# Sixteen merge-gate units projected in a phase of their own, by seven block products a pair, between the first net and attention

## The chip, the cores and the metric

The kernel runs on one core of a Trainium2 chip. The metric is the device time of one execution in microseconds (us). Below, PE is TensorE, ACT is ScalarE, DVE is VectorE, POOL is GpSimd and SP is SyncE, whose queue issues the kernel's DMAs. L526 is line 526 of the kernel before.

## The reference, cut to what matters

Two transformer blocks run over 1024 tokens of width 1024, in fp32. The first has a hybrid mixer (a state space part and retention) and a gated convolution net of width 2816. The second projects its input `x` once (`z = x @ w_in`) for three branches, gates them and ends in a second net:

```python
(qa, ka, va, qg, kg, vg, glr, gout, qh, fh, ih, hout, mg) = split_columns(x @ w_in)
oa = diff_attention(...)                  # 4 heads
ob = chunked_gated_linear_attention(...)  # GLA, 4 heads, log_g = log_sigmoid(...) / 16
log_f = logaddexp(log(max(lb, floor)), log1p(-lb) + log_sigmoid(fh)); k_h = -expm1(log_f)
oc = chunked_gated_linear_attention(qh, k_h, ih, log_f)   # HGRN, 4 heads
y = einsum('btnc,ncd->btnd', stack(oa, ob, oc), w_branch)
gates = sigmoid(mg.reshape(b, t, 3, 1024))
mix = einsum('btnd,btnd->btd', gates, y) @ w_out
```

`mg` is 3072 columns: 24 tiles of 128 columns by 1024 tokens, called gate units here. They depend on `x` alone, so they can be projected at any time before the branches are merged.

## The kernel before, in words

Every engine has its own program, written by hand and in order; semaphores join them. An fp32 product is three matmuls of cut operands: high by high, low by high and high by low. The cut of an input block is XH and XL. A weight unit of 512 KB goes through a ring: SP loads WR, ACT cuts the high half WH (L1520), POOL the low half WL (L3299), and PE waits for that.

A feature unit (L526) gives 128 columns for 1024 tokens: eight slices of six matmuls, 48 in all. The slices are a generator that `tick` advances, so they are laid between the steps of other work.

The two nets project their upper weights by pairs of units with seven block products instead of eight (`pe_up`, L971): the input is split by rows and tokens into quarters, seven sums and differences of quarters (TH and TL hold the combined ones, numbered 1 to 4) are multiplied by sums and differences of the two units' halves, and ACT and DVE add up the seven results (PC tiles). A pair costs 84 matmuls instead of 96. POOL makes the combined weights (L3333 to L3339) and their low cuts.

The order of the work around the change:

1. The first net's lower product ends with the layer norm of the eight token tiles of XF. DVE norms, ACT scales (L1752), POOL multiplies by the gain (L3353), PE turns XF by transposes (L601), ACT and DVE cut it out of PSUM to XH and XL (L1739, L2624). Then POOL adds the bias for the residual (L3358) and SP stores it.
2. `pe_open` (L867) projects the first head's q, k and v by half tokens, with the turns of x between them.
3. Attention: four heads of eight steps. A step has scores (L1252), transposes of the softmax weights (L1265) and outputs (L1282), and HEAD_TICKS says how many slices stand beside it. The slices are the next head's projections, then gate units from BESIDE_HEAD.
4. Six gated jobs: jobs 0 and 1 have two GLA heads each, jobs 2 to 5 one HGRN head each. A job has levels 0 to 6 of decayed products KQ by KQ (L1397, L1385; DVE makes KQ on L3154 and L3156 out of K, Q and the decays DD) and a diagonal, then eight chunks (state, output), and at last the transposes of the normed output YG (L1447). JOB_TICKS gives the slices before level 0, after each level and after each chunk; what is left is run by `finish(fill)` ahead of the YG transposes. Beside job j run the projections for job j+1: first its keys (ck), which for HGRN are also the forget gates, out of which ACT and DVE compute log_f (L2111, L2085, L2087; L3031, L3018, L3023, L3043); then the output gate of job j, q and v of job j+1, and the gate units of BESIDE_JOB.
5. The branch products, with the late gate units between them, then the output projection and the second net.

A gate unit done early is copied from PSUM to EG by ACT (L1528) and stored to DRAM; it is read back for its sigmoid later.

```python
pe_open(e, [(("dq", 0), "w_in_2", 0), (("dk", 0), "w_in_2", 512), ((("dv", 0), "x"), "w_in_2", 1024)])
...
    fill = chain(pe_gated_keys(e, j + 1), pe_gated_gates(e, j), pe_gated_project(e, j + 1), pe_early(e, BESIDE_JOB[j]))
    compute(j, fill, JOB_TICKS[j])
...
                    last.then_inc(c_o, 1)
                    tick(fill, per[2])
                finish(fill)
                bk.let(uo)
```

Of the kernel before, what the change touches and what calls it, by code (L numbers as in the profile page):

```python
# [294 lines left out]
def build(nc, D, out):  # L295
# [19 lines left out]
    with ExitStack() as ctx:  # L315
# [548 lines left out]
        def pe_half(e, u, wh, wl, h, beside={}):  # L864
            for k in range(8):
# [3 lines left out]
                for what, part in beside.get(k, ()):  # L869
                    pe_turn_pair(e, *what, part)  # L870
            return last

        def pe_open(e, units):

            us = []

            def begin(n):
                name, unit, col = units[n]
                v = wt.next(unit, 0, 8, col, 128)
                us.append((v, claim(e, name, 2, hold=True)))  # L880
# [6 lines left out]
            begin(0)
            pe_wait_pairs(e, "x2", (0, 1))
            first(0)
            begin(1)  # L890
            pe_turn_pair(e, "x2", 2, (0, 1, 2))
            first(1)
            pe_turn_pair(e, "x2", 2, (3,))
            bk.lend(lots["x2n"], ln_ab, chains_of["x2"] + 4)
            begin(2)
            pe_turn_pair(e, "x2", 3, (0, 1))
            first(2, {3: ((("x2", 3), (2,)),), 5: ((("x2", 3), (3,)),)})
            pe_wait_pairs(e, "x2", (2, 3))
# [50 lines left out]
        pair_at = {}  # L949
        COMBINED = ((2, 0), (1, 0), (2, 1), (1, 1), (4, 0), (4, 1), (3, 0), (3, 1))  # L950
# [27 lines left out]
        def pe_up(e, name, unit, source):  # L978
            f = ("f1", "f2").index(name)
# [50 lines left out]
            for n, c in enumerate(UP_COLS[name][0]):  # L1030
# [3057 lines left out]
```

## Time and profile before

| | us |
|---|---|
| three runs | 2848.1, 2844.63, 2841.9; median 2844.63 |
| profiled execution | 2844.59 |
| its span | 2842.8 |
| PE busy in the span | 2805.1 (99%) |
| the other engines | DVE 1759.4, POOL 1367.7, ACT 1147.7 |

The profiled execution lies at the median, and its span is 1.8 us shorter than its time. By PE's lines the stages are: mixer to 384 us, first net to 1034, opening of the second block to 1073.5, attention to about 1366, gated jobs to 1908.4, branches to 2108.4, output projection to about 2200, second net to the end.

### The profile page before, as it was taken

Reading aid. Unit: us, or ns where it says so; the run is one execution under the profiler, and the core shown is the slowest. Engines: PE = TensorE matmul, PEld = TensorE weight load, DVE = VectorE, ACT = ScalarE, POOL = GpSimd, SP = SyncE. Lnnn points to the kernel's source line nnn. Section 1 sums busy time; section 2 is a strip of 40 time slices with the busy share of each in tenths; the row PEclk is TensorE's granted clock in tenths of the full one; section 3 lists DMA queues with packets and bytes.
Section 4 is the critical chain, followed back from the end, with each engine's and each line's share of the span. In section 5 each row is a group of like instructions: output and inputs, shape, how many; then the busy total and the mean of one; then the engine's idle time right before and its main releaser. Section 6 shows DMA issues by size and latency. Waiting matters only on the chain.

```text
span 2842.8 us, 41241 instructions
## 1 busy us (share of the span) xinstructions
PE 2805.1 (99%) x16498; PEld 2300.2 (81%) x16498; DVE 1759.4 (62%) x2801; ACT 1147.7 (40%) x1681; POOL 1367.7 (48%) x690
## 2 busy tenths in 40 slices
PE   9999999999999999999999999999999999999998
PEld 8877888888888877777887888887888788888886
DVE  8848684555468776555536665522455766648776
ACT  4334364444443334333435554423233533433331
POOL 3543359977758662111211111212223799847774
PEclk9999999999999999999999999999999999999999
DMA  6351203333355322112101111125330244453441
GB/s 223 95 156 56 104 16 111 104 108 104 100 179 184 104 79 80 52 53 67 53 31 54 61 60 60 60 91 186 109 142 23 78 152 163 155 215 120 154 153 70
DMA packets 114318, 296.09 MB, mean 104 GB/s; under 512 B 14544, under 2 KB 23168, under 8 KB 114112
## 3 DMA queue, kind: packets, MB, share of 16 engines
q1 hardware_dynamic: 114128, 293.46, 30.5%
q8 instruction: 131, 2.15, 0.3%
q14 instruction: 59, 0.48, 0.1%
HBM read 216.61 MB, written 76.81 MB: 103 GB/s over the span
## 4 chain that ended last, share of the span: by engine, by line
PE 88%; DVE 4%; POOL 3%; ACT 2%; issue 2%; DMA 1%; SPq 0%; ACTq 0%; DVEq 0%; POOLq 0%
PE PS L526 29%; PE PS L971 21%; PE PS L1129 4%; PE PS L1128 4%; PE PS L1130 4%; PE PS L575 3%; PE PS L577 3%; PE PS L576 3%; POOL WL L3299 1%; PE PS L1252 1%; PE PS L1282 1%; PE PS L1385 1%; PE PS L1150 1%; PE PS L1148 1%; PE PS L1149 1%
## 5 line engine op out<-in xcount | busy, mean ns | idle before, releaser
L3299 POOL TENSOR_TENSOR WL<-WR,WH 128x1024 fp32r<-128x1024 f32 x236 | 585.1, 2484 | 1128.1 <-ACT WH L1520 1127.9
L1520 ACT ACTIVATE WH<-WR 128x1024 fp32r<-128x1024 f32 x237 | 248.7, 1054 | 285.3 <-POOL WR L3339 143.8
L526 PE MATMUL PS<-XH,WH 128*128 128x512 f32 x1040 | 338.8, 407 | 1.6 <-DVE XL L2312 0.9
L526 PE MATMUL PS<-XL,WH 128*128 128x512 f32 x1040 | 322.8, 391 | 1.3 <-issue 1.3
L526 PE MATMUL PS<-XH,WL 128*128 128x512 f32 x1040 | 321.3, 390 | 0.0
L971 PE MATMUL PS<-XH,WH 128*128 128x512 f32 x624 | 244.1, 391 | 5.1 <-DVE XL L2642 5.0
L971 PE MATMUL PS<-XH,WL 128*128 128x512 f32 x624 | 243.3, 390 | 0.0
L971 PE MATMUL PS<-XL,WH 128*128 128x512 f32 x624 | 243.3, 390 | 0.0
L526 PEld LDWEIGHTS PS<-XH,WL 128*128 128x128 f32 x1040 | 195.2, 188 | 44.7 <-issue 1.5
L526 PEld LDWEIGHTS PS<-XL,WH 128*128 128x128 f32 x1040 | 195.2, 188 | 42.7
L2857 DVE TENSOR_TENSOR XF<-XF,PS 128x512 f32<-128x512 f32 x280 | 185.8, 681 | 70.9 <-PE PS L1130 70.7
L3299 POOL TENSOR_TENSOR WL<-DW,WH 128x1024 fp32r<-128x1024 f32 x70 | 178.5, 2557 | 101.3 <-ACT WH L1520 99.4
L526 PEld LDWEIGHTS PS<-XH,WH 128*128 128x128 f32 x1040 | 182.2, 189 | 46.7 <-issue 14.9
L1128 PE MATMUL PS<-WH,XH 128*128 128x512 f32 x560 | 217.8, 389 | 0.0
L1129 PE MATMUL PS<-WL,XH 128*128 128x512 f32 x560 | 217.8, 389 | 0.0
L1130 PE MATMUL PS<-WH,XL 128*128 128x512 f32 x560 | 217.8, 389 | 0.0
L575 PE MATMUL PS<-WH,XH 128*128 128x512 f32 x480 | 189.2, 394 | 1.8 <-ACT KQT L1528 0.7
L577 PE MATMUL PS<-WH,XL 128*128 128x512 f32 x480 | 187.0, 390 | 0.0
L576 PE MATMUL PS<-WL,XH 128*128 128x512 f32 x480 | 186.9, 389 | 0.0
L971 PE MATMUL PS<-TH,WH 128*128 128x512 f32 x464 | 178.2, 390 | 1.0 <-DVE PC L2777 1.0
L971 PE MATMUL PS<-TH,WL 128*128 128x512 f32 x448 | 174.3, 389 | 0.0
L1520 ACT ACTIVATE WH<-DW 128x1024 fp32r<-128x1024 f32 x70 | 74.2, 1061 | 247.9 <-PE PS L1130 74.6
(418 smaller groups left out, 5932.7 us busy)
## 6 DMA issues: line engine op xcount, KB each, us to landing
WR<-in_weights SPq DMA_DIRECT2D x201, 512.0 KB, 3.5
HR<-hsum SPq DMA_DIRECT2D x70, 512.0 KB, 3.7
hsum<-CT SPq DMA_DIRECT2D x40, 512.0 KB, 3.1
DW<-in_weights SPq DMA_DIRECT2D x40, 512.0 KB, 6.3
hsum<-CT SPq DMA_DIRECT2D x40, 256.0 KB, 2.4
gates<-EG SPq DMA_DIRECT2D x18, 512.0 KB, 5.0
EI<-gates SPq DMA_DIRECT2D x18, 512.0 KB, 5.2
hbuf<-CT SPq DMA_DIRECT2D x14, 512.0 KB, 3.4
```

What stands on the lines that cost most here:

```text
L526: last = e.matmul(PS[:, u.b + h, :], w, x[:, k, 512 * h:512 * h + 512], start=k == 0 and w is w1 and x is xh, stop=k == nk - 1 and w is w2)
L575: e.matmul(PS[:, u.b, :], a, wh[:, k, :], start=j == 0 and k == 0, stop=False)
L576: e.matmul(PS[:, u.b, :], a, wl[:, k, :], start=False, stop=False)
L577: last = e.matmul(PS[:, u.b, :], c, wh[:, k, :], start=False, stop=j == len(vs) - 1 and k == 1)
L971: last = e.matmul(PS[:, u.b + at, :], a[:, k, :], b[:, k, :], start=start and k == 0 and a is w[0] and b is x[0], stop=stop and k == 3 and ...
L1128: e.matmul(o, a, wh[:, k, :], start=k == 0 and not added, stop=False, skip_group_check=added)
L1129: e.matmul(o, a, wl[:, k, :], start=False, stop=False, skip_group_check=added)
L1130: last = e.matmul(o, c, wh[:, k, :], start=False, stop=k == 1, skip_group_check=added)
L1148: e.matmul(o, a, wh[:, k % 2, :], start=k == 0, stop=False)
L1520: e.activation(WH[:, v % NSPL, :], raw_at(r), ACT.Copy).then_inc(w_hi, 1)
L2857: e.tensor_tensor(x, x, bank(u), ALU.add).then_inc(u.drained, 1)
L3299: e.tensor_tensor(WL[:, v % NSPL, :], raw_at(r), WH[:, v % NSPL, :].bitcast(F), ALU.subtract).then_inc(w_lo, 1)
```

## The change

The early gate units grow from 18 to 20. Sixteen of them (AHEAD) are projected in a new phase "g2" after the first net: two units whole, then seven pairs by seven block products. One unit is left beside attention (before 6) and three beside the gated jobs, all in job 5 (before 12). The tick tables shrink to match; job 0's stays.

```diff
-BESIDE_HEAD = [EARLY[0:1], EARLY[1:2], EARLY[2:3], EARLY[3:6]]
-BESIDE_JOB = [[], EARLY[6:7], EARLY[7:9], EARLY[9:11], EARLY[11:13], EARLY[13:18]]
-HEAD_TICKS = [(2, 3, 3, 4, 4, 5, 6, 7)] * 3 + [(1, 2, 2, 3, 3, 4, 4, 5)]
-
-JOB_TICKS = [(1, (4, 4, 3, 3, 3, 3, 3, 3), 1), (6, (4, 4, 4, 3, 3, 3, 3, 3), 1)] + [(5, (4, 4, 4, 4, 3, 3, 3, 3), 1)] * 4
+EARLY = [(0, pt) for pt in range(2, 8)] + [(n, pt) for n in (1, 2) for pt in range(1, 8)]
+AHEAD = EARLY[0:16]
+BESIDE_HEAD = [[], [], [], EARLY[16:17]]
+BESIDE_JOB = [[], [], [], [], [], EARLY[17:20]]
+HEAD_TICKS = [(1, 2, 2, 3, 3, 4, 5, 6)] * 3 + [(0, 1, 1, 2, 2, 3, 3, 3)]
+
+JOB_TICKS = [(1, (4, 4, 3, 3, 3, 3, 3, 3), 1), (4, (3, 3, 3, 3, 3, 2, 2, 2), 1)] + [(3, (3, 3, 3, 2, 2, 2, 2, 2), 1)] * 4
...
             pe_ffn(e, "f1", "ffn_w_up", "ffn_w_down", "x1", "x2")
+            pe_ahead(e)
             pe_diff(e)
...
+                "g2": [(gate_col(*AHEAD[m]), gate_col(*AHEAD[m + 1])) for m in range(0, len(AHEAD), 2)]}
```

Since the combined input tiles of "g2" are needed, x is now turned the way the nets turn theirs: raw copies out of PSUM, a high cut, differences, combined tiles. The gains of the last two token tiles go from POOL to DVE, and POOL adds the eight biases singly beside the seven pairs. The opening has no turns between its products any more; its second halves need the upper late quarter of XH and XL, whose room two combined tiles took, so SP stores that quarter (2 x 1 MB) to DRAM and reads it back during the last pair.

```diff
+            for p in range(1, len(UP_COLS["g2"])):
+                pool_cut_to(e, pair_at["g2", p] + 7)
+                for t in bias_beside[p]:
+                    pool_bias(e, "x2", t)
...
+            e.wait_ge(x_lo, row_count(1, 3, 1))
+            for k in range(2):
+                e.dma_start(D["xup"][k], upper_late[k][:, :, :].bitcast(F).rearrange("p k c -> p (k c)")).then_inc(x_sp, 16)
...
             if n in (3, 4):
                 e.wait_ge(x_u, f + 1)
+                if NETS[f] == "g2":
+                    e.wait_ge(x_sp, STORED)
             e.activation(TH[n][:, :, c], TR[n][:, :, c], ACT.Copy).then_inc(x_hi, 1)
...
                 e.wait_ge(w_lo, v + 1)
-                pe_half(e, u, *cut_of(v, 8), 0, beside)
...
+                pe_half(e, u, *cut_of(v, 8), 0)
+            e.wait_ge(x_bk, BACK)
             for v, u in us:
```

How the change moves instructions, at three places. First PE at the end of jobs 2 to 4, from the last chunk's output (VB, ST) to the YG transposes; every three rows of XH and XL are one slice. Before:

```order
L1436 MATMUL PS<-VB_199,ST 128x128
L526 MATMUL PS<-XH,WH 128x512 x2
L526 MATMUL PS<-XL,WH 128x512 x2
L526 MATMUL PS<-XH,WL 128x512 x2
...
L526 MATMUL PS<-XH,WH 128x512 x2
L526 MATMUL PS<-XL,WH 128x512 x2
L526 MATMUL PS<-XH,WL 128x512 x2
L1447 MATMUL PS<-ident,YG 128x128 x8
```

The "..." stands for six more slices. Now there is one slice in their place:

```order
L1429 MATMUL PS<-VB_194,ST 128x128
L536 MATMUL PS<-XH,WH 128x512 x2
L536 MATMUL PS<-XL,WH 128x512 x2
L536 MATMUL PS<-XH,WL 128x512 x2
L536 MATMUL PS<-XH,WH 128x512 x2
L536 MATMUL PS<-XL,WH 128x512 x2
L536 MATMUL PS<-XH,WL 128x512 x2
L536 MATMUL PS<-XH,WH 128x512 x2
L536 MATMUL PS<-XL,WH 128x512 x2
L536 MATMUL PS<-XH,WL 128x512 x2
L1440 MATMUL PS<-ident,YG 128x128 x8
```

Eight slices became three. Second DVE in the levels of such a job, around the keys and decays of the next one (KT_196 is its key tile, LG_197 its log decay, US_189 a helper; KT_191 and LG_192 are this job's). Before:

```order
L3128 TENSOR_TENSOR DD_170<-LG_192 128x1024
L3031 TENSOR_SCALAR KT_196<-KT_196,s_61 128x1024
L3018 SCALAR_TENSOR_TENSOR US_189<-LG_197 128x1024
L3154 TENSOR_TENSOR KQ<-KT_191,DD_171 128x32x16
L3156 TENSOR_TENSOR KQ<-QT_190,DD_171 128x32x16
L3085 COPY ST<-PS 32x8x32 x2
L3128 TENSOR_TENSOR DD_171<-LG_192 128x1024
L3023 SCALAR_TENSOR_TENSOR LG_197<-LG_197,US_189 128x1024
L3154 TENSOR_TENSOR KQ<-KT_191,DD_170 128x64x8
```

Now:

```order
L3183 TENSOR_TENSOR DD_171<-LG_192 128x1024
L3086 TENSOR_SCALAR KT_196<-KT_196,s_61 128x1024
L3073 SCALAR_TENSOR_TENSOR US_189<-LG_197 128x1024
L3209 TENSOR_TENSOR KQ<-KT_191,DD_170 128x64x8
L3211 TENSOR_TENSOR KQ<-QT_190,DD_170 128x64x8
L3162 COPY_PREDICATED STB_184<-LVB,PS 128x8x16
L3183 TENSOR_TENSOR DD_170<-LG_192 128x1024
L3078 SCALAR_TENSOR_TENSOR LG_197<-LG_197,US_189 128x1024
L3209 TENSOR_TENSOR KQ<-KT_191,DD_171 128x128x4
```

The same chain of the next job now starts at level 3 (64x8) instead of level 2 (32x16), and it stands in front of levels that have two slices behind them on PE instead of three or four. Third POOL at the end of the first net, from the gains of tiles 0 to 3 on. Before:

```order
L3353 TENSOR_TENSOR XF<-XF,LNG 128x1024 x4
L3299 TENSOR_TENSOR WL<-WR,WH 128x1024 x2
L3353 TENSOR_TENSOR XF<-XF,LNG 128x1024 x4
L3299 TENSOR_TENSOR WL<-WR,WH 128x1024 x2
L3358 TENSOR_TENSOR XF<-XF,LNB 128x1024 x8
```

Now:

```order
L3410 TENSOR_TENSOR XF<-XF,LNG 128x1024 x4
L3356 TENSOR_TENSOR WL<-WR,WH 128x1024 x2
L3390 TENSOR_TENSOR S_140<-WR 128x512
L3392 TENSOR_TENSOR WR<-WR 128x512
L3394 TENSOR_TENSOR WR<-S_140,WR 128x512
L3396 TENSOR_TENSOR WR<-WR 128x512
L3410 TENSOR_TENSOR XF<-XF,LNG 128x1024 x2
L3356 TENSOR_TENSOR WL<-WR,WH 128x1024
```

The combined weights of the first pair now stand ahead of the gains of tiles 4 and 5, and the biases are gone from here.

## Rows read from the trace of the kernel before

**Rows 1.** The page: span, and the first row of engine busy time

```profile
span 2842.8 us, 41241 instructions
PE 2805.1 (99%) x16498; PEld 2300.2 (81%) x16498; DVE 1759.4 (62%) x2801; ACT 1147.7 (40%) x1681; POOL 1367.7 (48%) x690
```

**Rows 2.** Windows by stage: busy us and count by engine, clock, DMA share, GB/s

```profile
1034.00:1073.50 39.50, 37.13 (x179) 30.03 (x178) 27.51 (x42) 16.71 (x26) 37.53 (x16) 1.00 0.42 154
1073.50:1366.00 292.50, 292.14 (x1500) 225.51 (x1500) 164.73 (x443) 121.30 (x263) 39.48 (x18) 1.00 0.17 58
1366.00:1908.40 542.40, 537.93 (x5806) 441.68 (x5805) 294.28 (x449) 263.61 (x463) 104.79 (x48) 1.00 0.18 58
```

**Rows 3.** The same view, 100 us in the first net's upper product

```profile
500.00:600.00 100.00, 100.00 (x443) 82.81 (x442) 56.82 (x54) 43.75 (x56) 87.66 (x49) 1.00 0.32 108
```

**Rows 4.** Waits of PE: what, total us, times, longest

```profile
PE PS L971 <- DVE XL L2642: 5.0, 2, 2.5
...
PE PS L1385 <- DVE KQ L3156: 1.7, 3, 0.6
```

**Rows 5.** Timeline of PE, opening: start, us, operation, count [idle before <-releaser]

```profile
1040.08 1.50 PE L601 MATMUL PS<-ident,XF 128*128 128x128 f32 x12 [0.43 <-POOL XF L3353]
...
1049.33 0.66 PE L601 MATMUL PS<-ident,XF 128*128 128x128 f32 x4 [1.40 <-DVE XL L2624]
...
1056.95 0.47 PE L867 MATMUL PS<-XH,WH 128*128 128x512 f32 x1 [0.54 <-DVE XL L2624]
```

**Rows 6.** Timelines of DVE and PE, third step of the fourth head

```profile
1280.91 1.28 DVE L2918 SCALAR_TENSOR_TENSOR PD<-PD,SMD 128x1024 f32<-128x1024 f32 x1
...
1282.85 1.09 PE L1265 MATMUL PS<-ident,PD 128*128 128x128 f32 x8
```

**Rows 7.** Timeline of ACT, job 3, from the end of the key unit

```profile
1678.10 1.28 ACT L2111 ACT_TABLE_LOAD   x1 [6.33 <-PE PS L526]
...
1685.71 1.28 ACT L2087 ACT_TABLE_LOAD   x1
1687.01 1.06 ACT L2087 ACTIVATE US<-US 128x1024 f32<-128x1024 f32 x1
```

**Rows 8.** Timelines of DVE, POOL and PE there

```profile
1680.52 0.81 DVE L3031 TENSOR_SCALAR KT<-KT,s 128x1024 f32<-128x1024 f32 x1 [4.86 <-ACT KT L2111]
1682.58 2.90 DVE L3154 TENSOR_TENSOR KQ<-KT,DD 128x512 f32<-128x512 f32 x1
1685.41 0.68 DVE L3156 TENSOR_TENSOR KQ<-QT,DD 128x512 f32<-128x512 f32 x1
...
1688.10 1.23 DVE L3023 SCALAR_TENSOR_TENSOR LG<-LG,US 128x1024 f32<-128x1024 f32 x1
...
1682.36 2.58 POOL L3299 TENSOR_TENSOR WL<-WR,WH 128x1024 fp32r<-128x1024 f32 x1 [12.39 <-ACT WH L1520]
...
1686.23 0.73 PE L1385 MATMUL PS<-KQ 128*32 128x16 f32 x64 [0.57 <-DVE KQ L3156]
```

**Rows 9.** Timelines of PE, DVE and POOL, end of job 3

```profile
1735.01 0.39 PE L1436 MATMUL PS<-VB,ST 128*128 128x128 f32 x2
...
1746.17 1.04 PE L1447 MATMUL PS<-ident,YG 128*128 128x128 f32 x8
...
1738.08 2.41 DVE L2273 TENSOR_SCALAR sm<-sm 128x8 f32<-128x8 f32 x3 [0.31 <-ACT YG L2201]
...
1740.52 0.17 DVE L2273 TENSOR_TENSOR sm<-sm 128x8 f32<-128x8 f32 x1
...
1742.33 1.29 DVE L3214 TENSOR_TENSOR YG<-PS,sm 128x512 f32<-128x512 f32 x2
...
1737.10 2.95 POOL L3299 TENSOR_TENSOR WL<-WR,WH 128x1024 fp32r<-128x1024 f32 x1 [14.78 <-ACT WH L1520]
```

**Rows 10.** Windows behind the two waits of PE at L971, columns as in rows 2

```profile
403.90:407.30 3.40, 2.90 (x7) 2.32 (x8) 3.40 (x4) 0.00 (x0) 0.00 (x0) 0.51 0.25 101
...
2221.40:2225.00 3.60, 3.58 (x16) 2.97 (x17) 3.56 (x4) 0.00 (x0) 0.00 (x0) 1.00 0.13 53
```

More of the change, by code:

```diff
@@ L149, in weight_plan @@
     o1 = ffn("ffn_w_up", "ffn_w_down", 22, UP_COLS["f1"])
+    for c in UP_COLS["g2"][0]:
+        feat("w_in_2", c)
+    for c in UP_COLS["g2"][1:]:
+        pair("w_in_2", *c)
     for h in range(4):
@@ L875, in pe_open @@
             us = []
-            def begin(n):
-                name, unit, col = units[n]
+            for name, unit, col in units:
                 v = wt.next(unit, 0, 8, col, 128)
-                us.append((v, claim(e, name, 2, hold=True)))
-            def first(n, beside={}):
-                v, u = us[n]
+                u = claim(e, name, 2, hold=True)
+                us.append((v, u))
                 e.wait_ge(w_lo, v + 1)
-                pe_half(e, u, *cut_of(v, 8), 0, beside)
[L887 to L898, printed above, removed]
+                pe_half(e, u, *cut_of(v, 8), 0)
+            e.wait_ge(x_bk, BACK)
             for v, u in us:
@@ L1806, in act_item, with counted, act_copy_block @@
             e.activation(item_cut(name, x)[0], item_raw(name, x), ACT.Copy).then_inc(f_hi, 1)
+        def counted(name, p):
+            return p + PAIRS_BEFORE[name]
+        def act_copy_block(e, name, n, what, p, s, free):
+            u = lots[name, what, p]
+            e.wait_ge(u.full, u.nfull)
+            if free and counted(name, p) > 1:
+                e.wait_ge(free, counted(name, p) - 1)
+            t = e.activation(PC[n][:, :], bank(u), ACT.Copy)
+            t.then_inc(u.drained, 1) if s is None else t.then_inc(s, 1)
@@ new lines, in act_ahead, with tile_out @@
+        def act_ahead(e):
+            n_pairs = len(UP_COLS["g2"])
+            L = lambda what, p: lots["g2", what, p]
+            def tile_out(m, u):
+                if m < 2:
+                    e.wait_ge(h_out[m], stored_at["f1", "all"][m])
+                    e.wait_ge(ln_g, ln_of["x2"] + 8)
+                else:
+                    e.wait_ge(e_out[m % 2], 16 * (m // 2))
+                e.activation(CT[m % 2][:, :], bank(u, 2), ACT.Copy).then_inc(u.drained, 1)
+            at = pair_at["g2", 1]
+            act_copy_block(e, "g2", 1, "A1", 1, None, f_b)
+            for d in range(2):
+                act_combined(e, 1, 2, d)
+                act_combined(e, 1, 1, d)
+            act_copy_block(e, "g2", 3, "E3", 1, None, f_t1)
+            act_cut_to(e, at + 2)
+            for n in (4, 3):
+                for d in range(2):
+                    act_combined(e, 1, n, d)
+            act_cut_to(e, at + 3)
+            for m in range(2):
+                u = L("first", m)
+                e.wait_ge(u.full, u.nfull)
+                tile_out(m, u)
+                if m == 0:
+                    act_cut_to(e, at + 4)
+            for p in range(1, n_pairs):
+                v = pair_at["g2", p]
+                act_cut_to(e, v + 4)
+                if p > 1:
+                    e.wait_ge(f_t2, counted("g2", p - 1))
+                    tile_out(2 * p - 1, L("G", p - 1))
+                    act_copy_block(e, "g2", 1, "A1", p, None, f_b)
+                    act_copy_block(e, "g2", 3, "E3", p, None, f_t1)
+                    act_cut_to(e, v + 6)
+                act_copy_block(e, "g2", 5, "E5", p, f_cp, f_t2)
+                if p > 1:
+                    act_cut_to(e, v + 7)
+                e.wait_ge(f_t1, counted("g2", p))
+                tile_out(2 * p, L("B", p))
+                act_copy_block(e, "g2", 4, "G", p, f_cp, None)
+                if p == 1:
+                    act_cut_to(e, v + 7)
+            e.wait_ge(f_t2, counted("g2", n_pairs - 1))
+            tile_out(2 * n_pairs - 1, L("G", n_pairs - 1))
@@ L2261, in scalar_program @@
             act_ffn(e, "f1", True, "x2")
+            act_ahead(e)
             act_diff(e)
@@ L3390, in pool_ffn @@
             if turned:
-                for t in (0, 2, 4, 6, 1, 3, 5, 7):
-                    pool_bias(e, turned, t)
+                pool_cut(e, u.units)
             else:
```

239 lines of the change are left out of this document (133 added, 106 removed).

## The prediction, made before the changed kernel had run

> **What bounds the kernel now.** I read the page's head first: PE is busy for 2805.1 of 2842.8 us [rows 1], so the kernel is as long as PE's list of instructions plus 38 us in which PE stands. Then the windows by stage: in attention PE is busy for 292.14 of 292.50 us, in the gated jobs for 537.93 of 542.40 [rows 2]. There the other engines are at half load (DVE 294.28, ACT 263.61 of 542.40), and their work is hidden because slices of projections lie between the dependent steps. Then PE's waits: the two nets each lose 2.5 us at their opening product, and the decay chain of the gated jobs already shows through three times with 0.6 us [rows 4]. The last is the reading that decides here: in jobs 2 to 4 the cover is used up at one level. The timelines of ACT, DVE and POOL behind that wait [rows 7, 8] and at the end of a job [rows 9] give the length of the two chains that the slices cover.
>
> **What goes away: matmuls.** The new order has 84 matmuls fewer in all: seven pairs at 84 instead of 96. In the first net's upper product, the same kind of work, 443 matmuls take 100.00 us [rows 3], so one is 0.2257 us and 84 are 19.0 us. The ends: the whole 19.0 is there if the seven-product phase runs as the net does; nothing in it waits more than 1.0 us in the nets apart from their opening. The same row gives a slice (six matmuls) as 1.36 us, which I use below; 16 units are moved, and their time is not gained by being moved.
>
> **The opening of the new phase.** Three waits go: 0.43, 1.40 and 0.54, together 2.4 us [rows 5], because the turns of x lie elsewhere. In their place comes the opening that both nets have, in which the third product waits 2.5 us for the differences [rows 4]. Here two things are later than in the nets: POOL now has the combined weights of the first pair ahead of the gains of tiles 4 and 5, and the turn of these tiles waits for them; and the gains of tiles 6 and 7 are on DVE, which is on the way to the same products. On POOL this is four halves of a cut ahead of two gains. I take a net +2 us; ends 0 (the nets' wait alone, and the three old ones gone) and +8 (the four half sums and two gains, at about 2.4 us for a full tile as POOL's cuts show [rows 8], all uncovered). The biases leave POOL's list here and go singly beside the pairs, where POOL is busy for 87.66 of 100 us [rows 3] in the net with the same cuts; one bias more in 18 us is hidden, since each net pair has its cuts ready ahead of PE.
>
> **The stored quarter.** 2 MB go out to DRAM before the combined tiles 3 and 4 may be written. In the opening of before the DMA engines moved 154 GB/s at a share of 0.42 [rows 2], that is 367 GB/s when full, so 2.1 MB take 5.7 us at best. The whole units of "g2" give PE about 96 matmuls, 21.7 us, and the first pair's early products follow. I cost the store at nothing, hidden behind these; if it starts 10 us late, it shows for some 6 us. Reading it back is asked for during the last pair, a good 10 us ahead of its use: nothing. The sixteen gate tiles are stored as before.
>
> **Attention.** It loses 5 units of 8 slices. Its waits have room of several us at most steps, since the scores of a step are made two steps ahead. The tightest is the fourth head's start: DVE ends the weights of that step at 1282.19 and PE turns them at 1282.85 [rows 6], 0.66 us of room, and the new table takes two slices, 2.7 us, out ahead of it. So PE waits 2.0 us there. I take +2; ends 0 and +6 (the same at three heads).
>
> **The gated jobs, levels.** Twelve units fall to three, and none is left in jobs 1 to 4. PE has 16 slices, 21.8 us, less to lay between the steps of jobs 2, 3 and 4. The clock of the argument is A, the start of the table load that follows the next job's key unit (1678.10 in [rows 7]). Before, KQ of the level behind it is ready at A + 8.13, at 1686.23, with 0.57 us of PE waiting [rows 8]; the way there is the table load, the copy of KT, DVE's scale and difference, and a KQ of 2.90 us beside POOL's cut. After, the same instructions stand in the same row ahead of level 3. PE reaches level 3 after one slice, level 2 (0.7) and three slices: A + 6.2. It waits 1.9 us. Level 4 hangs on ACT's US, which ends at 1688.07, A + 9.97 [rows 7], the log sum of 1.23 us behind it [rows 8] and two KQ of 0.68 less overlap: A + 12.4. PE is there two slices after level 3, at A + 11.7: 0.7 us. Level 5 has six DVE tile operations ahead of its KQ pair (decay difference, key product, two scales, helper, and the mask), some 5.5 us by their rows' kind, and the pair 1.2: A + 19.2 against A + 16.2, 3.0 us. Level 6 hangs on the second US through ACT's three instructions (3.4 us), the sum and the pair: A + 23.8 against A + 22.9, 1.0 us. That is 6.6 us per job; less the 0.57 that goes, 6.0 in each of jobs 2, 3 and 4, 18 us, and for job 1, which keeps four slices before level 0, I take 1.5. The ends: 6 us (only level 3 waits, since a late level gives the chain time) and 22.
>
> On DVE's rows: the KQ on L3154 took 2.90 us while POOL's cut of 2.58 us ran, and its twin on L3156 took 0.68 [rows 8]. The Trainium skill, SBUF — State Buffer, "Who interferes with whom", says that a DVE instruction with two SBUF inputs contends with a POOL instruction that reads SBUF; the trace agrees. By that rule each POOL cut that leaves a job would give back 2.2 us, two per job; the cut behind the key unit stays where it was, so I take nothing from it for level 3.
>
> On ACT's rows: a table load takes 1.28 us and the next instruction starts 0.02 us after it [rows 7]. The Trainium skill, ScalarE: Activation LUTs, "What ACT_TABLE_LOAD costs", puts a switch at about 2.66 us with a drain. By the page three switches would make the chain some 4 us longer; the trace's 1.3 decides.
>
> **The gated jobs, ends.** The last chunk's output ends at 1735.40, the YG transposes start at 1746.17 [rows 9]: 10.8 us, eight slices. YG is ready at 1743.62, so 8.2 us after the chunk. With three slices PE has 4.0 us (three times 1.36 less what the last chunk overlaps). Of the 8.2, the three small operations at 1738.08 took 2.41 us beside POOL's cut, where an undisturbed one takes 0.17; that cut is no longer there, so YG is ready after 6.3: a wait of 2.3 us in each of jobs 2, 3 and 4, and for job 5 half of it, 8.0 together. Ends: 4 and 16 (the 8.2 stays: 4.2 each).
>
> **Granted clock.** After the first net's wait of 2.5 us [rows 4], at 404, the next 3.4 us had a granted clock of 0.51, the lower of the two levels, 1.2 GHz; after the second net's, at 2221, it stayed at 1.00 [rows 10]. Each fall costs half of 3.4 us, 1.7. Some eight of my new waits are 2 us or more; I take two falls, +3; ends 0 and +10.
>
> **Sum.** -19.0 (matmuls) + 2 (opening) + 2 (attention) + 19.5 (levels) + 8 (job ends) + 3 (clock) = +15.5 us. Against the profiled execution's 2844.59 us that is 2860.1; that execution lies on the median of 2844.63, so I predict 2860 us.
>
> **The rivals.**
>
> (a) *The matmuls are gained, the cover holds.* The decay chain could be shorter than I make it (fewer POOL cuts beside it, each late level giving the rest time), so that the levels wait 3 us in all and the job ends 2 or 3. For it: DVE has 294 and ACT 264 us of 542, and PE waits there for 4.5 us only [rows 2]. Against it: the 0.57 us with four slices behind each level, where two will be. Time: 2844.6 - 19 + 2 + 0 + 3 + 2.5 = 2833. This is the other side: one mechanism, the chain of the next job's decays against the slices before levels 3 to 6. It decides where the chain is 5 us shorter per job than I read it.
>
> (b) *Half is exposed.* The levels wait but the job ends do not, or the other way about: 19.5 or 8 of the 27.5, with no clock falls. About 2844.6 - 19 + 4 + 14 = 2844, between 2839 and 2850.
>
> (c) *More is exposed.* The clock falls after each of the waits (+10 instead of +3) and the store of the quarter holds up the first pair (+6): 2860 + 13 = 2873.
>
> (d) *The change does not do what it says.* The order shows 84 matmuls fewer, so only a phase that waits for its cuts could undo it: 19 us more than (a), 2852. It is within (b) and the forecast.
>
> **Chances.** The forecast (2851 to 2868) 0.58, (a) 0.15, (b) 0.14, (c) and beyond 0.13. A measurement of this kernel can tell 0.2%, 5.7 us, from no change: faster is under 2838.9, slower over 2850.3. Faster: nearly all of (a) 0.14. Same: most of (b) 0.13. Slower: the rest, 0.73. The range takes in all but the tails of (a) and (c): 2834 to 2876; the forecast's own range is 2851 to 2868.
>
> **What the changed profile would show.** Right: PE's busy time falls by about 19 us to 2786 and the time rises nevertheless; PE's waits for KQ grow from 1.7 us to about 20, and a wait of the YG transposes for YG, four times about 2 us, is new; the gated jobs take about 472 us instead of 542.4 (nine units of 10.9 us less, 27.5 more). The opening of the new phase shows one wait for the differences of 2.5 to 5 us. Wrong: gated jobs of 450 us, which is rival (a); a wait of PE on a combined tile of the new phase with the store as releaser, which is (c); and any wait of more than 1 us per pair for combined weights, which no row of before speaks for.

## The result: 1.6% slower, and where the 42 us went

The changed kernel takes 2889.93 us (median of four runs, 2886.3 to 2891.9) against 2843.57 of the kernel before on the same chip: a ratio of 1.0159, 95% interval 1.0141 to 1.0177. Slower was forecast, but the size was not: 15.5 us were predicted, 46 came, and 2890 lies above the range. All the traces below are of single executions. That of the changed kernel is the fastest of its four, with 2886.31 us, so its span accounts for 42 of the 46 us; the other three had a lower mean clock (0.988 to 0.990 against 0.991).

The page of the profiled execution (span 2884.5, so 41.7 us more than before) answers to [rows 1]:

```profile
span 2884.5 us, 41294 instructions
PE 2805.1 (97%) x16414; PEld 2298.2 (80%) x16414; DVE 1767.4 (61%) x2830; ACT 1186.2 (41%) x1737; POOL 1425.0 (49%) x730
```

PE has the 84 matmuls fewer (16414 against 16498), and yet it is busy for the same 2805.1 us. So two things happened: PE stands 41.7 us longer, and what it does takes as long as before with less to do. The windows by stage (new phase and opening, attention, gated jobs, branches), columns as in [rows 2], show both:

```profile
1036.90:1234.50 197.60, 193.52 (x860) 159.54 (x858) 67.60 (x114) 85.47 (x112) 131.59 (x70) 0.99 0.39 142
1234.50:1493.30 258.80, 245.25 (x1260) 186.07 (x1260) 155.51 (x420) 112.21 (x254) 26.59 (x12) 0.97 0.13 44
1493.30:1976.00 482.70, 450.55 (x5374) 366.99 (x5373) 278.44 (x448) 241.56 (x441) 80.86 (x39) 0.98 0.14 45
1976.00:2151.20 175.20, 175.20 (x774) 144.81 (x773) 83.11 (x56) 57.03 (x58) 38.46 (x16) 1.00 0.43 150
```

The clock column was 1.00 in attention and in the gated jobs [rows 2]; it is 0.97 and 0.98 now, and PE's idle time grew from 0.4 to 13.6 us and from 4.5 to 32.2. By PE's own rows the stages compare like this; "moved" is the slices that left or came, at 10.86 us a unit of eight, "waits" is what PE's idle time grew by, and "clock" is half of the time at the lower level, less the same of before:

| stage | before | after | moved | left over | waits | clock |
|---|---|---|---|---|---|---|
| end of the first net | 1034.2 | 1036.9 | 0 | +2.7 | +2.6 | 0 |
| new phase and opening | 39.3 | 197.7 | +154.7 | +3.7 | +1.7 | +1.7 |
| attention | 291.1 | 257.4 | -54.3 | +20.6 | +13.2 | +6.8 |
| gated jobs | 542.9 | 483.2 | -97.7 | +38.0 | +27.7 | +10.2 |
| branches | 200.8 | 175.2 | -21.7 | -3.9 | -2.2 | -1.7 |
| output projection, second net | 721.6 | 721.6 | 0 | 0 | -0.9 | +1.7 |

(The new phase's 154.7 is 16 units less 19.0 for the 84 matmuls.) The saving is there: with the 19.0 counted as saved, 61.1 us are left over, and waits and clock, read by themselves, come to 60.8. 61.1 less 19.0 is the 42.1 by which PE's last matmul is later.

PE's waits, columns as in [rows 4]:

```profile
PE PS L1378 <- DVE KQ L3211: 19.8, 11, 2.8
PE PS L1440 <- DVE YG L3269: 7.0, 4, 2.0
PE PS L961 <- DVE XL L2681: 6.4, 3, 2.5
PE PS L1258 <- DVE SMD L2958: 5.9, 3, 3.6
PE PS L1258 <- ACT VD L1983: 3.9, 1, 3.9
PE PS L1363 <- issue: 3.3, 1, 3.3
PE PS L611 <- POOL XF L3410: 3.2, 2, 2.5
PE PS L611 <- DVE XF L2931: 2.5, 1, 2.5
PE PS L1258 <- DVE PD L2971: 2.5, 1, 2.5
```

The first two are the gated jobs' and were forecast (L1385 and L1447 before). Job 2's levels 3, 4 and 5 and its end stand where the prediction put them, for 1.9, 0.7, 3.0 and 2.3 us (here and below, only those rows of a timeline that waited):

```profile
1728.27 0.73 PE L1378 MATMUL PS<-KQ 128*32 128x16 f32 x64 [1.85 <-DVE KQ L3211]
1732.73 0.73 PE L1378 MATMUL PS<-KQ 128*32 128x16 f32 x64 [0.79 <-DVE KQ L3211]
1739.24 1.05 PE L1378 MATMUL PS<-KQ 128*32 128x16 f32 x64 [2.82 <-DVE KQ L3211]
...
1773.85 1.06 PE L1440 MATMUL PS<-ident,YG 128*128 128x128 f32 x8 [2.02 <-DVE YG L3269]
```

Jobs 3 and 4 repeat them. The three rows on L1258 are new. The 2.5 us is the wait in the fourth head that was forecast with 2.0; the other two rows were not forecast. What stands behind the 3.6 us, from DVE's timeline in head 0:

```profile
1249.92 0.15 DVE L3017 TENSOR_TENSOR s<-cols 128x4 f32<-128x4 f32 x1
1253.50 0.18 DVE L3019 RECIPROCAL s<-s 128x4 f32<-128x4 f32 x1 [3.42 <-ACT s L2077]
1253.71 2.31 DVE L2324 TENSOR_TENSOR s<-s 128x4 f32<-128x4 f32 x2
...
1257.00 0.17 DVE L3027 TENSOR_SCALAR s<-s 128x4 f32<-128x4 f32 x1 [0.37 <-ACT s L2080]
1257.15 0.82 DVE L2958 CUSTOM_DVE_ANT_0 PD<-PS,AL 128x640 f32<-128x640 f32 x1
```

Small work of another stage (the tables of the lower bounds, a column of four) stands in DVE's list between two steps of the softmax. It waits 3.4 us for ACT, which first copies the unit that PE has just ended and cuts a weight. Two of the small operations then take 2.31 us. The reader of the scores (L2958) behind them starts at 1257.15, and PE had ended these scores at 1252.8, so it starts 4.3 us later than they allow. In head 3 the norm of the previous head's output stands ahead of the reader in the same way.

The clock, columns as in [rows 2], behind six of the waits of 2.0 us or more:

```profile
1257.60:1261.10 3.50, 3.06 (x9) 2.58 (x10) 3.14 (x10) 2.40 (x5) 0.00 (x0) 0.51 0.24 95
1738.90:1742.30 3.40, 3.06 (x69) 2.67 (x70) 1.32 (x3) 3.35 (x4) 0.00 (x0) 0.51 0.02 5
1773.80:1777.20 3.40, 3.35 (x19) 2.96 (x20) 2.25 (x3) 2.44 (x3) 0.88 (x1) 1.00 0.00 0
1807.20:1814.00 6.80, 5.96 (x76) 4.79 (x76) 4.71 (x8) 6.17 (x6) 0.49 (x1) 0.50 0.01 2
1844.70:1848.10 3.40, 3.40 (x12) 2.72 (x10) 2.87 (x4) 1.67 (x2) 1.65 (x1) 0.51 0.00 0
1879.80:1883.20 3.40, 3.39 (x76) 2.81 (x76) 1.31 (x3) 3.37 (x3) 0.00 (x0) 1.00 0.00 0
```

Of 15 waits of PE of 2.0 us or more from 400 us on, eleven are followed by such a fall to the lower level (1.2 GHz) and four are not. A twelfth fall, at 1479.5, has no wait in front of it. Shorter waits can have one too: in e11 below, a wait of 1.86 us at 1730.6 is followed by one. Two waits of the same length and place, 2.82 at 1808 and 2.85 at 1880, came out at 0.50 for 6.8 us and at 1.00.

### The profile page after: what moved, and what is told of

The parts are those of the page before. It is cut to its first block, busy times and chain, and to the rows that moved or that the text cites. A ratio compares the mean times of both kernels' runs of the same rounds, so it can differ in the third digit from the quotient of the medians.

```text
span 2884.5 us, 41294 instructions
## 1 busy us (share of the span) xinstructions
PE 2805.1 (97%) x16414; PEld 2298.2 (80%) x16414; DVE 1767.4 (61%) x2830; ACT 1186.2 (41%) x1737; POOL 1425.0 (49%) x730
## 4 chain that ended last, share of the span: by engine, by line
PE 82%; DVE 6%; ACT 4%; POOL 4%; issue 3%; DMA 1%; SPq 0%; DVEq 0%; ACTq 0%; POOLq 0%
PE PS L961 27%; PE PS L536 21%; PE PS L1121 4%; PE PS L1123 4%; PE PS L1122 4%; PE PS L585 3%; PE PS L587 3%; PE PS L586 3%; POOL WL L3356 2%; PE PS L1245 1%; PE PS L879 1%; PE PS L1275 1%; PE PS L1378 1%; PE PS L611 1%; PE PS L1258 1%
## 5 line engine op out<-in xcount | busy, mean ns | idle before, releaser
L3356 POOL TENSOR_TENSOR WL<-WR,WH 128x1024 fp32r<-128x1024 f32 x243 | 601.8, 2481 | 1111.2 <-ACT WH L1518 1110.9
L961 PE MATMUL PS<-XH,WH 128*128 128x512 f32 x760 | 298.5, 393 | 6.7 <-DVE XL L2681 6.4
L961 PE MATMUL PS<-XL,WH 128*128 128x512 f32 x760 | 297.3, 391 | 0.0
L961 PE MATMUL PS<-XH,WL 128*128 128x512 f32 x760 | 297.3, 391 | 0.0
L536 PE MATMUL PS<-XH,WH 128*128 128x512 f32 x784 | 263.8, 418 | 2.3 <-ACT QT L1526 1.0
L536 PE MATMUL PS<-XL,WH 128*128 128x512 f32 x784 | 247.6, 397 | 0.0
L536 PE MATMUL PS<-XH,WL 128*128 128x512 f32 x784 | 245.1, 394 | 0.0
L961 PE MATMUL PS<-TH,WH 128*128 128x512 f32 x564 | 215.6, 389 | 0.0
L961 PE MATMUL PS<-TH,WL 128*128 128x512 f32 x540 | 210.1, 389 | 0.0
L961 PE MATMUL PS<-TL,WH 128*128 128x512 f32 x516 | 200.7, 389 | 0.0
L1812 ACT ACTIVATE PC<-PS 128x512 f32<-128x512 f32 x172 | 102.0, 593 | 193.3 <-PE PS L961 192.1
L536 PEld LDWEIGHTS PS<-XL,WH 128*128 128x128 f32 x784 | 150.2, 192 | 33.6
L536 PEld LDWEIGHTS PS<-XH,WL 128*128 128x128 f32 x784 | 149.6, 191 | 34.2 <-issue 0.3
```

The costliest lines, as they stand in the source:

```text
L536: last = e.matmul(PS[:, u.b + h, :], w, x[:, k, 512 * h:512 * h + 512], start=k == 0 and w is w1 and x is xh, stop=k == nk - 1 and w is w2)
L961: last = e.matmul(PS[:, u.b + at, :], a[:, k, :], b[:, k, :], start=start and k == 0 and a is w[0] and b is x[0], stop=stop and k == 3 and ...
L1812: t = e.activation(PC[n][:, :], bank(u), ACT.Copy)
L3356: e.tensor_tensor(WL[:, v % NSPL, :], raw_at(r), WH[:, v % NSPL, :].bitcast(F), ALU.subtract).then_inc(w_lo, 1)
```

## The experiments

All times are medians, beside the kernel before on the same chip (2844.1, 2843.3 and 2844.5 us in the three sets); the changed kernel, from the measurement above, is 2889.9 us beside 2843.6. e1 to e3, e6 and e7 also spread the eight biases over fewer pairs. My theory after the trace: attention and the gated jobs are bound by chains on DVE and ACT as soon as the slices between their steps run out, each wait of 2 us or more costs again through the clock, and the matmuls saved are real. The rivals: the waits come from what else moved (loads, biases, the later start), or they are single places that better laid slices would mend.

### e1: attention's units put back

```diff
-AHEAD = EARLY[0:16]
+AHEAD = EARLY[0:10]
-BESIDE_HEAD = [[], [], [], EARLY[16:17]]
-BESIDE_JOB = [[], [], [], [], [], EARLY[17:20]]
+BESIDE_HEAD = [EARLY[10:11], EARLY[11:12], EARLY[12:13], EARLY[13:16]]
+BESIDE_JOB = [[], [], [], [], [], EARLY[16:20]]
-HEAD_TICKS = [(1, 2, 2, 3, 3, 4, 5, 6)] * 3 + [(0, 1, 1, 2, 2, 3, 3, 3)]
+HEAD_TICKS = [(2, 3, 3, 4, 4, 5, 6, 7)] * 3 + [(1, 2, 2, 3, 3, 4, 4, 5)]
```

> The changed kernel with attention's cover put back: 10 units in the new phase (4 pairs by seven), six beside the heads (1, 1, 1, 3) with the old HEAD_TICKS, four beside job 5; the other jobs as in the changed kernel. Theory (attention's loss is cover, and the clock falls that its waits bring): attention gives back the 20.6 us that it lost beyond the moved units (12.6 of waits, some 7 of clock), three pairs fewer cost 3 x 12 matmuls, 8.1 us; so 2890 - 13 = about 2877, with no wait over 1 us on the softmax weights. Rival (the waits come from the moved loads or the later start of attention, not from the slices): the waits of 2 to 4 us stay, about 2898.

Measured: 2880.7 us. The stage of attention, as in [rows 2]:

```profile
1179.60:1472.10 292.50, 292.13 (x1500) 225.49 (x1500) 159.41 (x429) 121.38 (x262) 38.63 (x17) 1.00 0.17 57
```

292.13 busy of 292.50 at a clock of 1.00: to 0.01 us the stage of before, though it starts 106 us later with the loads where the change put them. The rival is out: it was the slices. The whole is 4 us above the sum's 2877: in the gated jobs, whose lists are those of the changed kernel but for one unit, the clock takes 17.1 us in this profile instead of 10.2. How many falls there are differs from one execution to the next.

### e2: the gated jobs' units put back

```diff
+AHEAD = EARLY[0:8]
+BESIDE_HEAD = [[], [], [], EARLY[8:9]]
+BESIDE_JOB = [[], EARLY[9:10], EARLY[10:12], EARLY[12:14], EARLY[14:16], EARLY[16:20]]
+JOB_TICKS = (that of the kernel before)
```

> The changed kernel with the gated jobs' cover put back: 8 units in the new phase (3 pairs by seven), eleven beside jobs 1 to 5 (1, 2, 2, 2, 4) with the old JOB_TICKS, one beside the fourth head. Theory (gated loss of 38 us is cover and clock): 38 back, four pairs fewer cost 48 matmuls, 10.8 us; about 2863, with PE's waits for KQ at 2 us in all. Rival (the chain is longer for another reason): the waits stay, about 2900.

Measured: 2878.0 us, 15 above the theory's number. Jobs 2 to 4:

```profile
1642.60:1888.10 245.50, 243.52 (x2376) 199.43 (x2375) 144.69 (x211) 131.57 (x213) 48.27 (x21) 1.00 0.19 61
```

They take 245.5 us (before: 245.6), with waits for KQ of 1.7 us in all, as [rows 4]. The theory holds there. Most of the 15 us is two mistakes of the edit: job 5 had four units with ticks for five, so that no slice was left ahead of its YG transposes (and the clock was at the lower level for 10.2 us around it),

```profile
PE PS L1440 <- DVE YG L3269: 7.7, 1, 7.7
...
PE PS L961 <- POOL WL L3356: 2.9, 2, 2.7
```

and three biases a pair on POOL held up the new phase's cuts by 2.7 us. In the trace a wait of 2.7 us in job 1, for which the profile names no releaser, and 2.2 us in the first net (see e11) come on top. The first mistake is a measurement of its own: with no cover YG is 7.7 us behind the last chunk.

### e3: one unit beside each of jobs 1 to 4

```diff
+AHEAD = EARLY[0:12]
+BESIDE_JOB = [[], EARLY[13:14], EARLY[14:15], EARLY[15:16], EARLY[16:17], EARLY[17:20]]
+JOB_TICKS: job 1 as before; jobs 2 to 4 (4, (4, 4, 4, 3, 3, 3, 2, 2), 1)
```

> The changed kernel with one gate unit beside each of jobs 1 to 4 (12 units in the new phase), JOB_TICKS of jobs 2 to 4 at (4, (4, 4, 4, 3, 3, 3, 2, 2), 1), job 1 with the old ones. Cover theory: job 1 gives back its two waits and two clock falls (9 us), jobs 2 to 4 the waits at levels 3 and 4 and most of level 5 and the end; two pairs fewer cost 5.4 us; about 2870. If the waits don't depend on the slices: 2895.

Measured: 2872.9 us, 3 above the theory's number. Its waits in the gated jobs are down from 19.8 and 7.0 us:

```profile
PE PS L1378 <- DVE KQ L3211: 11.4, 6, 2.2
...
PE PS L1440 <- DVE YG L3269: 2.9, 4, 0.9
```

With the other runs this gives the price of cover in jobs 2 to 4, a third of the time from the YG transposes of job 1 to those of job 4: with two units a job takes 81.9 us, with one 77.0, with none 70.2. The unit that leaves first frees 4.9 us, the next 6.8, and each costs 9.5 in the new phase (84 matmuls for two). So the two moves lose 7.3 us a job and 22 us in the three, with the saved matmuls already counted and the clock falls of these executions in them. Without any fall a job with no unit takes 68.8 us (e10 below), and the two moves still lose 5.9.

### e4: spare matmuls in front of the waits

```diff
+        def warm(e, b, *key):
+            for _ in range(WARM.get(key, 0)):
+                e.matmul(PS[:, b, :], XH[:, 0, 0:128], XH[:, 0, 0:512], start=True, stop=True)
...
                     if n < 7:
+                        warm(e, us[0].b, "l", j, n)
                         e.wait_ge(c_kq, 7 * j + n + 1)
```

> The changed kernel with spare matmuls (a block of x by itself, 512 columns, 0.226 us each) put in front of the longest waits of attention and the gated jobs, into the bank that the waiting step overwrites; their number is 0.2 to 0.4 us less than each wait (for example 15 before a wait of 3.63 us, 7 and 11 at levels 3 and 5, 8 before the YG transposes). They add 197 matmuls that compute nothing needed, in time in which PE stood. Theory (a wait costs twice: the wait and a clock fall behind it): nine falls of 1.7 us go, about 2875. Rival (the falls come from something else than PE's standing still, or the waits alone are the price): the time stays at 2890 or rises a little.

Measured: 2893.5 us, 3.6 above the changed kernel: as a whole it is the rival's number. (The kernel has 164 spare matmuls; the 197 of the expectation is a wrong count.) By place it says more. In attention the step waits for its PSUM bank and not for the weights, so the spare matmuls (L1232) came behind the wait and were simply added:

```profile
1259.07 6.33 PE L1232 MATMUL PS<-XH 128*128 128x512 f32 x15 [3.63 <-DVE SMD L2970]
```

The stage is 9.9 us longer. In jobs 2 to 4 they did what they should: no fall of the clock where the changed kernel has four, and the three jobs take 207.0 us instead of 210.6, though PE has 29 to 33 matmuls more in each. Job 3:

```profile
1787.10:1855.70 68.60, 66.35 (x723) 53.58 (x723) 44.58 (x70) 39.00 (x67) 10.65 (x5) 1.00 0.12 40
```

So the falls in these jobs hang on PE's standing still, and four of them, 6.8 us by the column, are worth 3.6 us. All four executions of e4 agree, with a mean clock of 0.993 to 0.995 against 0.988 to 0.991. The fall at 1479.5, without a wait, is not explained by this.

### e9, e10: the same slices, laid elsewhere

```diff
-HEAD_TICKS = [(1, 2, 2, 3, 3, 4, 5, 6)] * 3 + [(0, 1, 1, 2, 2, 3, 3, 3)]
+HEAD_TICKS = [(1, 2, 2, 3, 7, 4, 3, 2)] + [(1, 2, 2, 3, 3, 4, 5, 6)] * 2 + [(0, 2, 1, 4, 1, 4, 2, 1)]      (e9 alone)
...
-JOB_TICKS = ... + [(3, (3, 3, 3, 2, 2, 2, 2, 2), 1)] * 4
+JOB_TICKS = ... + [(3, (3, 3, 3, 2, 3, 2, 2, 1), 1)] * 4      (e9)
+JOB_TICKS = ... + [(2, (3, 3, 4, 2, 3, 2, 2, 1), 1)] * 4      (e10)
```

> The changed kernel, same units and same number of slices in each stage, laid elsewhere: jobs 2 to 5 get a third slice between levels 4 and 5, taken from behind level 7; head 0 gets two slices more ahead of the weights' transposes that waited 3.63 us (ticks (1, 2, 2, 3, 7, 4, 3, 2)), head 3 one more ahead of each of its three late ones ((0, 2, 1, 4, 1, 4, 2, 1)). Theory (each wait is a local lack of cover): the level 5 wait falls from 2.8 to 1.5 us in each of three jobs, attention's four waits from 11.9 to about 5, and the clock falls behind them go: about 2876. Rival (each stage is bound by its chain as a whole, so that a wait taken away here comes back at the next step): the waits move and the time stays within 4 us of 2890.

> The changed kernel with JOB_TICKS of jobs 2 to 5 at (2, (3, 3, 4, 2, 3, 2, 2, 1), 1): a slice more ahead of level 3 and of level 5, one less ahead of level 0 and behind level 7. Local cover: levels 3, 4 and 5 wait 5.5 us in the changed kernel, here about 2.5, with the falls of the clock fewer: 9 to 14 us less, 2879. Chain as a whole: the time stays at 2890, as the waits come back at level 6 or at the end of the job.

Measured: 2881.1 and 2885.5 us, which lies between the numbers of theory and rival both times. PE's waits in the levels of job 3 of e10:

```profile
1799.16 0.73 PE L1378 MATMUL PS<-KQ 128*32 128x16 f32 x64 [1.86 <-DVE KQ L3211]
1803.62 0.73 PE L1378 MATMUL PS<-KQ 128*32 128x16 f32 x64 [0.79 <-DVE KQ L3211]
1810.12 0.73 PE L1378 MATMUL PS<-KQ 128*32 128x16 f32 x64 [1.46 <-DVE KQ L3211]
1814.91 0.73 PE L1378 MATMUL PS<-KQ 128*32 128x16 f32 x64 [1.11 <-DVE KQ L3211]
```

Level 5's wait shrinks by the slice (2.82 to 1.46) and level 6 then waits 1.1; level 3's 1.86 does not move, because the slice put ahead of it went behind the one taken from level 0 and the key unit ends as close to level 3 as it did. PE's waits per job sum to the same: 8.0 us here, 7.8 in the changed kernel. In attention of e9 they are 13.0 us against 13.5: the 3.6 at head 0 is 0.9 now, and a new one of 3.5 stands at head 3. The chain as a whole sets the waiting, which was the rival. What did get shorter is the clock's part, which the rival's numbers left out: the mean clock is 0.993 to 0.994 in e9 and 0.991 to 0.993 in e10. The same job with the same matmuls, in the changed kernel and in e10:

```profile
1773.90:1844.00 70.10, 62.27 (x694) 50.08 (x694) 44.58 (x70) 38.93 (x67) 10.61 (x5) 0.95 0.13 39
```

```profile
1775.90:1843.90 68.00, 59.95 (x694) 48.42 (x694) 44.38 (x70) 38.89 (x67) 10.62 (x5) 1.00 0.13 40
```

694 matmuls in both, idle for 7.8 and 8.1 us, and 2.1 us apart: 0.95 against 1.00 of the clock. That is the price of the lower level in this job, 2.1 us where the column says 3.4. Over jobs 2 to 4 together, in which e10 has no fall, it is 4.2 us (210.5 against 206.35) where the column says 6.8.

### e11: the decay chain made shorter

```diff
             def decay(u):
-                softlog(u)
-                yield
...
+                for _ in range(2):
+                    logs.up()
+                    e.wait_ge(g_u, logs.n)
+                    e.activation(u, u, ACT.Copy, scale=1e-4).then_inc(g_l, 1)
+                    yield
```

> The changed kernel in which the log decays of jobs 3 to 5 (prepared in jobs 2 to 4) and of job 2 leave out part of the computation: the Exp and Ln of both softplus steps on ACT are one scaled copy, which takes away two activations of 1.06 us and up to four table loads of 1.28 us per job; all counts, tiles and the other engines' lists stay. Theory (levels 4 to 6 wait for this chain): the waits at level 4 (0.8) and 6 go, level 5's 2.8 shrinks to 1.5 or less since it is DVE's own list behind level 4, level 3's 1.85 stays; with the clock falls some 8 to 12 us less, about 2880. Rival (the levels wait for DVE's list alone): 2889.

The kernel leaves out the Exp and Ln of both steps of the log decays. Measured: 2884.4 us, between the two numbers. The waits of the levels of job 3:

```profile
1797.39 0.73 PE L1378 MATMUL PS<-KQ 128*32 128x16 f32 x64 [1.85 <-DVE KQ L3213]
1807.70 1.05 PE L1378 MATMUL PS<-KQ 128*32 128x16 f32 x64 [2.82 <-DVE KQ L3213]
```

Level 4's 0.79 is gone, so it was ACT's Exp, table load and Ln. In jobs 3 and 4 levels 3 and 5 stay to 0.01 us (in job 2 the clock falls behind level 3, and level 5 then waits 1.40 instead of 2.82): they wait for DVE's own list, level 3 through the 2.9 us KQ beside POOL's cut and level 5 through six tile operations. I had let level 5 shrink; it did not. DVE's list ahead of level 3, from the changed kernel:

```profile
1723.50 1.23 DVE L3073 SCALAR_TENSOR_TENSOR US<-LG 128x1024 f32<-128x1024 f32 x1
1724.65 2.88 DVE L3209 TENSOR_TENSOR KQ<-KT,DD 128x512 f32<-128x512 f32 x1
1727.45 0.68 DVE L3211 TENSOR_TENSOR KQ<-QT,DD 128x512 f32<-128x512 f32 x1
...
1724.42 2.56 POOL L3356 TENSOR_TENSOR WL<-WR,WH 128x1024 fp32r<-128x1024 f32 x1 [15.57 <-ACT WH L1518]
```

2.88 us against 0.68 for the twin: the difference of 2.2 us is more than the wait of 1.85. So level 3 should hardly wait if POOL's cut of the weights behind the key unit ran elsewhere; that is an estimate from these rows. The Trainium skill, SBUF — State Buffer, "Who interferes with whom", gives the rule for it (two SBUF inputs on DVE against a POOL instruction that reads SBUF), and this row agrees. No run tried it.

The trace of e11 shows one thing more about the clock, in the first net, whose instructions are the same in every kernel here. Everywhere PE waits 2.5 us there at its opening product, at about 404 us. In e2, e7 and e11 no fall follows, in the other ten traces one does. The first window of [rows 10] is the kernel before, with 0.51. The same window in e11, and what e11 has later:

```profile
403.90:407.30 3.40, 2.41 (x11) 2.00 (x12) 3.40 (x4) 0.36 (x1) 0.00 (x0) 1.00 0.36 136
...
429.12 0.50 PE L961 MATMUL PS<-TH,WH 128*128 128x512 f32 x1 [2.17 <-DVE PC L2779]
```

The three without a fall there have this new wait of 2.1 to 2.2 us at 429, and from the opening product to the turns behind the net they take 621.2 to 621.5 us. The ten with the fall don't have it and take 619.2 to 619.3. So the same net is 2 us longer in the executions without the fall. Nothing here varies the fall alone, but half of the time at the lower level is plainly not what a fall costs: with a slower PE a later wait can be missing.

### e5 to e8: the parts that could pay

e5 is the kernel before with 20 early units, the two moved to job 5. e6 is the new phase with the six units that needed no cover. e7 and e8 add one line, to e6 and to the changed kernel:

```diff
-        beside_down, copied_down = {(1, 4): 0, (0, 7): 1}, {(0, 6): 0, (0, 7): 1}
+        beside_down, copied_down = {(1, 4): 0, (0, 7): 1}, {(1, 4): 0, (0, 7): 1}
```

> The kernel before with one part of the change alone: 20 early gate units instead of 18, so that four late ones are left beside the branches instead of six; the two that move stand beside job 5 (seven instead of five), with the old ticks. No new phase, no matmul saved. Theory: the branches lose a wait of 2.16 us and the clock fall of 1.7 us behind it, as they did in the changed kernel (its branches are 25.5 us shorter, 21.7 of it two units): about 2840. Rival (the wait there went for another reason, the new gate order or the shorter jobs): 2844.

> The new phase with only those units whose place needed no cover: 6 units ahead (two pairs by seven), one from each of heads 1 and 2, two from job 5, two from the branches; one beside head 0, three beside head 3 and 1, 2, 2, 2, 3 beside jobs 1 to 5 with the old ticks there; seven of the eight biases behind the last pair on POOL. Sum against the kernel before: 24 matmuls -5.4, branches -3.9, opening of the phase +6.4 with its clock fall, job 5 +1: about 2842, no wait over 1 us in attention and none over 0.6 in jobs 2 to 4. Rival (the phase costs more than its opening, for example by POOL's biases or the stored quarter): 2850.

> The same with one line more: the copy and cut of the first turned pair of token tiles stands behind the residual sum of block (1, 4) on ACT and DVE instead of in front of it. Theory (the opening's two waits of 2.5 us come from DVE's order: the sum that frees a bank, and the statistics that lead to the next gains, stand behind two cuts that wait for ACT): both shrink, with the clock fall, 4 to 6 us less than the run before, about 2837. Rival (they come from POOL's two gains of 4.7 us, or the pair sums ahead of these): no difference, 2842.

> The changed kernel with that one line. By the theory the waits of 2.53 and 2.52 us in front of the turns shrink: 2890 - 5 = about 2885. By the rival (POOL's gains or pair sums): 2890.

| | us | ratio to before, interval |
|---|---|---|
| e5 | 2840.5 | 0.9994 (0.9985 to 1.0003) |
| e6 | 2845.5 | 1.0007 (0.9998 to 1.0016) |
| e7 | 2844.8 | 1.0006 (0.9997 to 1.0015) |
| e8 | 2891.2 | 1.0170 (1.0156 to 1.0184) |

e5: the wait ahead of the branches is 0.68 us instead of 2.16 and no fall follows it (one stands at the second net's opening instead); 24.9 us less in the branches, 21.8 more in job 5. Its 2840.5 is the theory's number and the best here, but its interval does not tell it from the kernel before; the missing wait in the trace does the telling. e6: attention's waits sum to 1.2 us and jobs 2 to 4 are at 81.4 to 82.8, as meant, and the whole comes out at no change, 3.5 us above the sum's 2842: two pairs save 5.4 us, and the new opening costs 6.2 in this trace. It waits there:

```profile
1024.16 0.63 PE L611 MATMUL PS<-ident,XF 128*128 128x128 f32 x4 [0.66 <-POOL XF L3410]
1027.32 2.82 PE L611 MATMUL PS<-ident,XF 128*128 128x128 f32 x12 [2.53 <-DVE XF L2931]
1045.04 1.94 PE L611 MATMUL PS<-ident,XF 128*128 128x128 f32 x16 [1.17 <-POOL XF L3410]
1062.57 0.50 PE L961 MATMUL PS<-XH,WH 128*128 128x512 f32 x1 [2.80 <-DVE XL L2681]
```

and e7 in the same place:

```profile
1026.53 1.94 PE L611 MATMUL PS<-ident,XF 128*128 128x128 f32 x16 [0.65 <-POOL XF L3410]
1037.23 0.47 PE L961 MATMUL PS<-XH,WH 128*128 128x512 f32 x1 [0.57 <-DVE XL L2675]
1047.36 3.65 PE L611 MATMUL PS<-ident,XF 128*128 128x128 f32 x16 [4.43 <-POOL XF L3410]
1065.53 0.50 PE L961 MATMUL PS<-XH,WH 128*128 128x512 f32 x1 [0.83 <-DVE XL L2681]
```

The line took away the wait of 2.53, as expected, and the one at the next gains grew from 1.17 to 4.43: a chain again, and my reason for the second wait (DVE's order) was wrong. The opening's waits sum to 6.5 us instead of 7.2, and the 2837 that I expected did not come. e8 says the same of the changed kernel: the 2.53 is gone, the wait at the gains is 4.41 instead of 2.52, and its 2891.2 is the rival's number.

## Why the prediction failed, step by step

- **Matmuls, -19.0:** right; there are 84 fewer, and only with 19.0 us saved do waits and clock (60.8) account for what is left over (61.1).
- **Opening, +2:** +6.4 with one clock fall, inside the ends of 0 and +8. I had laid it to POOL's pair sums ahead of the gains. They end 1.7 us before ACT's scaled tile lets the gains start; the waits are of the turns' own chain, two of 2.5 us.
- **The stored quarter, 0:** right; no wait has it as releaser.
- **Levels and job ends, +27.5:** right; the waits grew by 27.7 us, and e2, e3 and e11 show their cause. Part of the close sum is luck, since errors cancel in it. Levels of 1.85, 0.79, 2.82 and (in job 4) 1.11 stood against 1.9, 0.7, 3.0 and 1.0, ends of 2.0 against 2.3. The 1.1 of level 6, put down for three jobs, came in one. Job 1 was worse than the 1.5 put down: 5.9 us of waits against 2.5 before.
- **Attention, +2:** this step failed. I looked for the tightest place among the steps' own chains, and it waits 2.5 of the 13.2 us that came; with the clock the stage lost 20.6. Most of the rest are waits in places where I took several us of room for granted, and where DVE's list holds work of another head or stage whose input comes late. Before, one or two slices more per step hid that; e1 shows that the slices are what counts.
- **Granted clock, +3:** this step failed too, and has the largest miss in the sum: half the time at the lower level grew by 18.7 us. I took two falls for eight waits, from a pair of rows of which one had a fall; it was eleven for fifteen, and there were more waits than I had counted. As a price the 1.7 a fall was also wrong, the other way: in jobs 2 to 4 it is about 1 us, because the next wait takes a part back, and in the first net the executions with a fall are the shorter ones. The number outweighs this: the half time that was added is that of eleven falls, where I took two.
- **Branches, 0:** 3.9 us better; the wait of 2.16 and its fall went with the shorter stage, as e5 shows alone.
- Of the rivals, (c) had the mechanism (more exposed, the clock behind each wait) at 2873; it had no term for attention, and its term for the store did not come.
- Of the signs, the fall of PE's busy time to 2786 did not come, since the lower clock took the 19 us; the waits for KQ (19.8) and YG (7.0, four times) and the sign for the store were right.

What stays open: why one wait of 2.8 us brings a fall and its twin none. No run here varies that alone. What a stage loses without any fall is shown for jobs 2 to 4 only (e10); for attention no run separates waits and falls.

## What to carry to other kernels

Work laid between dependent steps is worth what it hides. Before moving it to a place where it is cheaper, find what a job takes with two, one and none of its pieces: here 81.9, 77.0 and 70.2 us, so a piece of 10.9 us frees 4.9 or 6.8 and must cost less than that elsewhere, where it costs 9.5. Room read at a step counts only if everything ahead in that engine's list is ready too, so read the list and not the step. And expect the clock to fall behind most waits of 2 us or more on TensorE, but take the price of a fall from two traces of the same stage and not from the column.

## What was not expected of the hardware

- Falls of the clock are not a fixed function of the wait: jobs 3 and 4 of one execution have the same list and the same wait of 2.8 us, and one has 6.8 us at half the clock behind it, the other none.
- A fall need not lengthen a stage: the first net takes 619.2 to 619.3 us in ten executions with one behind its opening wait, and 621.2 to 621.5 in three without, where PE meets another wait.
- PE busy with matmuls that compute nothing needed is cheaper than PE standing: 29 to 33 of them stood in the waits of each of three jobs, and the three were 3.6 us shorter. Placed behind the waits, in attention, 48 of them cost 9.9 us.
- Waits that sum to the same can cost differently: 8.1 us of them with none over 2.1 made a job of 68.0 us, 7.8 with one of 2.8 a job of 70.1. The clock, at 1.00 and 0.95, is the difference.
